# Low parts of the weights in four pieces, each with its own count, in a three-layer block kernel

## The reference, cut

```python
def reference(x, ...):
    h = rms_norm(x); proj = h @ w_in                 # pool, lru, q, k, v, three gates
    merged = g0 * (pool_mixer @ wb0) + g1 * (rglru_mixer @ wb1) + g2 * (stick_breaking_attention @ wb2)
    x = x + merged @ w_out
    x = x + (silu(rms_norm(x) @ w_gate) * (rms_norm(x) @ w_up)) @ w_down           # 1024 -> 2816 -> 1024
    # second model, layer 0: differential and block attention; layer 1: dilated and latent attention
    for layer in range(2):
        x = x + mixer(rmsnorm(x) @ w_in_layer) @ w_out_layer
        u, g = split(rmsnorm(x) @ ffn_w_in)
        x = x + (gelu(causal_conv3(g) + b) * u) @ ffn_w_out
    return rmsnorm(x)
```

## Time and profile before

| | us |
|---|---|
| three runs | 2345.93, 2337.33, 2343.05 |
| their median | 2343.05 |
| profiled execution, whole | 2347.11 |
| profiled execution, span of the trace | 2344.4 |
| PE busy | 2258.4 (96%) |
| POOL busy | 933.6 (40%) |
| DVE busy | 951.5 (41%) |
| ACT busy | 836.8 (36%) |
| granted TensorE clock, mean | 0.988 |

### The profile page before, as it was taken

The page is one execution under the profiler, slowest core; times in us unless marked ns, Lnnn a source line. Parts: engine busy times, 40 slices in busy tenths (PEclk is TensorE's granted clock), DMA queues, the critical chain, the costliest instruction groups (busy, mean ns, idle before and its releaser), DMA issues.

```text
span 2344.4 us, 27313 instructions
## 1 busy us (share of the span) xinstructions
PE 2258.4 (96%) x10130; PEld 1816.1 (77%) x10130; DVE 951.5 (41%) x1261; ACT 836.8 (36%) x1101; POOL 933.6 (40%) x264
## 2 busy tenths in 40 slices
PE   6999999899999999999988999999998999999997
PEld 4777877788878888888866778888886777888885
DVE  5244366634461111341156643233424546332334
ACT  4326465323232222331154333332323534333321
POOL 3331233443434344554421334436544123444453
PEclk9999999999999999999999999999998999999998
DMA  3221122222222322232321222222332112222232
GB/s 145 89 90 54 54 73 90 90 97 101 90 90 89 107 89 80 98 109 90 108 63 28 72 87 92 90 90 86 110 117 85 32 53 83 97 100 89 80 99 73
DMA packets 32701, 202.80 MB, mean 87 GB/s; under 512 B 3900, under 2 KB 4156, under 8 KB 13692
## 3 DMA queue, kind: packets, MB, share of 16 engines
q1 hardware_dynamic: 29932, 192.94, 23.8%
q0 software_dynamic: 2704, 8.97, 1.4%
HBM read 199.74 MB, written 2.15 MB: 86 GB/s over the span
## 4 chain that ended last, share of the span: by engine, by line
issue 53%; PE 30%; POOL 13%; DVE 1%; DMA 1%; ACT 0%; POOLq 0%; DVEq 0%; SPq 0%; ACTq 0%; PEldq 0%
POOL w_low L824 13%; PE bank L299 8%; PE bank L301 8%; PE bank L300 8%; PE bank L496 2%; PE bank L473 2%; PE bank L483 1%; DMA raw<-wmain 0%; PE bank L469 0%; PE bank L468 0%; POOLq L214 0%; DVE qk L1290 0%; DMA distance_table<-table 0%; PE bank L778 0%; PE bank L325 0%
## 5 line engine op out<-in xcount | busy, mean ns | idle before, releaser
L824 POOL TENSOR_TENSOR w_low<-raw,w_high 128x2048 fp32r<-128x2048 f32 x194 | 895.6, 4617 | 1249.3 <-ACT w_high L934 1236.9
L299 PE MATMUL bank<-x_low,w_high 128*128 128x512 f32 x1728 | 678.6, 393 | 17.2 <-DVE x_low L1283 9.2
L301 PE MATMUL bank<-x_high,w_low 128*128 128x512 f32 x1728 | 674.8, 391 | 0.0
L300 PE MATMUL bank<-x_high,w_high 128*128 128x512 f32 x1728 | 674.8, 390 | 0.0
L934 ACT ACTIVATE w_high<-raw 128x2048 fp32r<-128x2048 f32 x192 | 366.8, 1911 | 536.9 <-PE bank L301 532.8
L299 PEld LDWEIGHTS bank<-x_low,w_high 128*128 128x128 f32 x1728 | 325.5, 188 | 91.0 <-issue 20.0
L300 PEld LDWEIGHTS bank<-x_high,w_high 128*128 128x128 f32 x1728 | 325.7, 188 | 68.5 <-issue 1.2
L301 PEld LDWEIGHTS bank<-x_high,w_low 128*128 128x128 f32 x1728 | 325.5, 188 | 68.0
L299 PE MATMUL bank<-act_low,w_high 128*128 128x512 f32 x528 | 209.0, 396 | 1.3 <-POOL w_low L824 1.3
L301 PE MATMUL bank<-act_high,w_low 128*128 128x512 f32 x528 | 208.7, 395 | 0.0
L300 PE MATMUL bank<-act_high,w_high 128*128 128x512 f32 x528 | 208.6, 395 | 0.0
(11 more groups left out here) (239 smaller groups left out, 2458.8 us busy)
## 6 DMA issues: line engine op xcount, KB each, us to landing
raw<-wmain SPq DMA_DIRECT2D x146, 1024.0 KB, 4.8
raw<-wdown SPq DMA_DIRECT2D x48, 704.0 KB, 4.1
bias<-distance_table POOLq DMA_DIRECT2D x28, 256.0 KB, 3.4
x_residual<-x SPq DMA_DIRECT2D x2, 1024.0 KB, 6.1
out<-qk SPq DMA_DIRECT2D x8, 256.0 KB, 2.0
matrices<-mats SPq DMA_DIRECT2D x1, 512.0 KB, 9.9
r_blocks<-rg POOLq DMA_DIRECT2D x1, 512.0 KB, 6.4
i_blocks<-rg POOLq DMA_DIRECT2D x1, 512.0 KB, 7.0
```

What stands on the lines that cost most here:

```text
L299: pe.matmul(target, sh, ml, start=start and k == 0, stop=False)
L300: pe.matmul(target, sh, mh, start=False, stop=False)
L301: last = pe.matmul(target, sl, mh, start=False, stop=stop and k == n - 1)
L824: pool.tensor_tensor(wl[:, c, :], raw[:, c, :], wh[:, c, :].bitcast(F32), ALU.subtract).then_inc(low_ready, 1)
```

## The change

A constant `PIECES = 4` is new. POOL makes the low part of a chunk in four instructions, each with an increment of `low_ready`: of 512 columns each in a main chunk, of 384, 384, 384 and 256 in a down chunk. The first two chunks of each down stage are made in the last round of the stage ahead, as full ones with pieces of 512. All waits on `low_ready` count in pieces. PE waits for a piece where the first product of a chunk comes to it: every 2 steps in a main chunk, every step in a token-major one, every 3 in a down chunk. The second product of a chunk (`j` = 1, or the later token blocks) waits for none. The stage `qk` and the two chunks of `mla` still wait for the whole chunk through `chunk`. ACT's copy is 1408 columns wide where the chunk is a down chunk. The number of matmuls, loads and bytes is the same.

```diff
-                        sp_.wait_ge(low_ready, i * 2 + (n0 + c - 1))
+                        sp_.wait_ge(low_ready, i * (2 * PIECES) + PIECES * (n0 + c - 1))
...
                 for k, ((sh, sl), (mh, ml)) in enumerate(zip(stationary, moving)):
+                    if arrive and k % arrive[2] == 0:
+                        piece(arrive[0], arrive[1], k // arrive[2])
                     pe.matmul(target, sh, ml, start=start and k == 0, stop=False)
...
+            def piece(i, n, p):
+
+                pe.wait_ge(low_ready, i * PIECES + (PIECES * n + p + 1))
+
             def chunk(i, n):
-                pe.wait_ge(low_ready, i + (n + 1))
+
+                piece(i, n, PIECES - 1)
...
                 def part(i, n, c, x, read, x_ready=None):
-                    chunk(i * 2, n0 + 2 * n + c)
...
-                        products(bank[2 * c + j][:, :], weights(c, j), x).then_inc(sem(ready), 1)
+                        products(bank[2 * c + j][:, :], weights(c, j), x,
+                                 arrive=None if j else (i * 2, n0 + 2 * n + c, 2)).then_inc(sem(ready), 1)
...
-                chunk(0, BASE["mix"] + n)
                 for g in range(2):
                     f = 4 * c + 2 * g
+                    piece(0, BASE["mix"] + n, g)
...
-            def low(i, n, c):
+            def low(i, n, c, width=S):
 
                 pool.wait_ge(high_ready, i + (n + 1))
-                pool.tensor_tensor(wl[:, c, :], raw[:, c, :], wh[:, c, :].bitcast(F32),
-                                   ALU.subtract).then_inc(low_ready, 1)
+                for p in range(PIECES):
+                    part = slice(p * width, min((p + 1) * width, CHUNK if width == S else DOWN))
+                    pool.tensor_tensor(wl[:, c, part], raw[:, c, part], wh[:, c, part].bitcast(F32),
+                                       ALU.subtract).then_inc(low_ready, 1)
...
-                act.activation(wh[:, c, :], raw[:, c, :], ACT.Copy).then_inc(high_ready, 1)
+                act.activation(wh[:, c, 0:width], raw[:, c, 0:width], ACT.Copy).then_inc(high_ready, 1)
```

More of the change, by code:

```diff
@@ L333, in token_scales, with both_columns @@
                 last.then_inc(sem("token_scales"), 1)
-            def both_columns(c, x, read, target, ready, x_ready, at=0):
+            def both_columns(c, x, read, target, ready, x_ready, at, n):
                 for j in range(2):
@@ L340, in both_columns @@
                     pe.wait_ge(sem(x_ready[0]), x_ready[1] + k + 1)
+                    if k % 2 == 0:
+                        piece(0, n, k // 2)
                     for j in range(2):
@@ L356, in tiles @@
                     pe.wait_ge(sem(read), i * 4 + (2 * n + j + 1))
-                    products(bank[first + 2 * c + j][:, :], weights(c, j), x).then_inc(sem(ready), 1)
-                chunk(0, n0)
-                both_columns(0, x, read, first, ready, x_ready)
+                    products(bank[first + 2 * c + j][:, :], weights(c, j), x,
+                             arrive=None if j else (i * 2, n0 + n, 2)).then_inc(sem(ready), 1)
+                both_columns(0, x, read, first, ready, x_ready, 0, n0)
                 if norm:
                     norm_sum(norm)
-                chunk(0, n0 + 1)
                 tiles(0, 1, 1, 0)
@@ L403, in part @@
                 def part(i, n, c, x, read, x_ready=None):
[L404 removed]
                     if x_ready:
[L406 removed]
+                        both_columns(c, x, read, 2 * c, ready, x_ready, at, n0 + 2 * n + c)
                         return
@@ L430, in down @@
                         for c in range(2):
-                            chunk(i * 4, n0 + 2 * j + c)
                             pe.wait_ge(sem(x_ready), n * FT + (c + 1) * HALF)
                             products(bank[j][:, :], weights(c, 0, HALF, P), x[c * HALF:(c + 1) * HALF],
-                                     start=c == 0, stop=c == 1).then_inc(sem(ready), 1)
+                                     start=c == 0, stop=c == 1, arrive=(i * 4, n0 + 2 * j + c, 3))\
+                                .then_inc(sem(ready), 1)
             def turn(v, units, y_token):
@@ L574, in _ @@
                         last = products(bank[b][:, :], [(h[:, tokens], l[:, tokens]) for h, l in x], w,
-                                        start=c == 0, stop=c == 1)
+                                        start=c == 0, stop=c == 1,
+                                        arrive=None if b else (0, BASE["v"] + 2 * i + c, 1))
                         if c == 1 or b == NB - 1:
@@ L631, in column @@
                 n = MIX.index((kind, t // 2))
-                chunk(0, BASE["mix"] + n)
                 for k in range(KT):
+                    if t % 2 == 0 and k % 2 == 0:
+                        piece(0, BASE["mix"] + n, k // 2)
                     if x_ready:
@@ L830, in stage @@
                 rounds = count // 2 - (1 if n0 + count > CHUNKS else 0)
-                for i in repeat(pool, rounds):
-                    for c in range(2):
-                        low(i * 2, n0 + c, c)
+                down = count // 2 - 1 if name.startswith("down") else 0
+                if down:
+                    for i in repeat(pool, down):
+                        for c in range(2):
+                            low(i * 2, n0 + c, c, 3 * P)
+                if rounds > down:
+                    for i in repeat(pool, rounds - down):
+                        for c in range(2):
+                            low(i * 2, n0 + 2 * down + c, c)
             def query(kind, u0, i, n, u):
```

15 lines of the change are left out of this document (6 added, 9 removed).

## The result

| | before | after |
|---|---|---|
| median of the runs, us | 2342.38 (2337.33 to 2345.93, 4 runs) | 2323.62 (2320.39 to 2325.48, 4 runs) |
| profiled execution, us | 2347.11 | 2321.84 |
| span of its trace, us | 2344.4 | 2320.1 |
| mean granted clock in it | 0.988 | 0.993 |

The ratio of after to before is 0.992, with a 95% interval of 0.9897 to 0.9943. The predicted time was 2323.2 us. Between the medians lie 18.8 us, between the two spans 24.3, since the profiled execution of before was 4.7 us over its median and that of after 1.8 under.

The account below looks back on a forecast made before the run. PE, busy 96% of the span, bounds the kernel, so only its work and stalls can be won. Pieces 12.4 + DVE 5.4 + clock 2.6 - 0.6 = 19.8 us, giving 2323.2 us, range 2311 to 2335.

Parts of the forecast that it names:

- Gate and up entries: Second chunk pair of the three gate and up stages: PE's stalls for POOL's low part all go, 7.2 us.
- Down entries: First chunk of the three down stages: PE's stalls for POOL, each 0.6 us, all go, 1.8 us.
- A piece: POOL's time for a quarter of a chunk's low part: 1.23 us, with a fixed part of 0.10 us.
- a piece isn't a quarter: Rival, POOL's pieces: a fixed part of 1.4 us makes a piece 2.2 us; about 2350 us, chance 0.04.
- Pool products: Second chunk of the pool products: 3.4 us from the first piece, 1.5 us from DVE's chain ahead of ACT's copy.
- `x_low`: End of the three output projections: PE's waits for DVE's `x_low` go, 1.8 us (0 to 1.8).
- The start: Before PE's first product: two DVE operations slowed beside POOL gain 1.0 us (0 to 2.6).
- Dilated attention: DVE's operations behind POOL, for which PE stands, gain 1.1 us (0 to 3.4).
- The clock: Half-clock stretches after the third gate and up entry (1.6) and the pool products (1.0) go: 2.6 us (0 to 3.6).
- DVE comes first: Rival: back-to-back DVE operations keep the port, POOL takes what is left; 29 us gained, 2314 us, chance 0.20.
- Pieces alone: Rival: DVE stays blocked through all four pieces and clock dips stay; 11.8 us gained, 2331 us, chance 0.20.
- The waits show: Rival: PE's about 550 added waits hold up matmuls in gate, up and down loops; 2369 us, slower, chance 0.06.

Follow-up runs that it names:

- the repeat: The changed kernel run again unchanged, as the mark for the other runs: 2321.9 us, ratio 0.991 to the kernel before.
- Experiment 4: The changed kernel, but POOL makes a first piece, then the rest of the chunk in one instruction: 2331.78 us, ratio 0.9957 to the kernel before.
- experiment 3: The changed kernel with POOL's four pieces, but PE waits for the last piece of a chunk everywhere: 2346.13 us, ratio 1.0015 to the kernel before.
- experiment 1: The changed kernel with all of PE's new waits, but POOL makes each low part in one instruction: 2343.34 us, ratio 1.0001 to the kernel before.
- early high part: The changed kernel, but ACT makes the second pool product chunk's high part before its last `y_high` copy: 2321.39 us, ratio 0.9908 to the kernel before.

## Why the prediction was right, point by point

The forecast was the likeliest case, and it happened: PE starts on the first piece, and DVE gets turns. The sum without the clock's term was 17.2 us, and at an equal clock 16 were measured; the clock was worth 3 to 5 instead of 2.6. That the predicted median was met to 0.4 us is luck in part: these two errors cancel, and the middle of four runs shifts by 2 us with their clock (the repeat had 2321.9). Term by term, by how much earlier PE passes the same matmul in the two traces:

- **Gate and up entries**, predicted 7.2: 2.3, 2.7 and 2.6, together 7.6. **Down entries**, predicted 1.8: 0.7 each, 2.1. Right. Experiment 4 adds what the sum took for granted: it is not enough that a first piece is early, the following ones must come at PE's pace of 1.36 us. Without that, 3.8 us of waits come back.
- **A piece**, estimated at 1.23 us, took 1.29, and 384 columns 1.02, not 0.95. From 256, 384 and 512 columns (0.74, 1.02, 1.29) the fixed part comes to 0.19 us, not the 0.10 of a memset. The rival "a piece isn't a quarter" needed 1.4.
- **Pool products**, predicted 3.4 + 1.5 = 4.9: 4.5. The size is right, the remaining wait is not what I said. "PE's wait for `w_low`, 2 to 5 us, all before the pool products" is there with 3.7 us, but for `y_low` from DVE. I had not looked at what else PE needs at that matmul.
- **`x_low`** at the output projections, predicted 1.8: 0.7 each, 2.1, a little over what I took as the most; the 1.3 us of waits are gone. Right, and experiments 3 and 4 show that it is the turns. L1336's mean, which I gave as the sign of it, is a poor one: in experiment 4 it is 0.96 us, lower than in the changed kernel, and PE waits as before.
- **The start**, predicted 1.0 gained: 0.3 lost. This is the one term with the wrong sign. I wrote myself that a DVE chain without gaps wins little if they take turns, and then still took 1.0 for it. Each of the three instructions had to wait for a piece.
- **Dilated attention**, predicted 1.1: 1.5 (the wait for `probs` fell from 6.3 to 4.8). The first instruction took 1.34 us instead of 4.58, but the two behind it 3.42 instead of 1.69: each of them now waited for a piece.
- **The clock**, 2.6: the 1.6 after the third entry came. Of the 1.0 after the pool products 0.4 came, as the stall stayed at 3.7 us. The premise, that without a stall nothing pulls the clock down, holds at the gate and up entries. Whether more stalls gone explain the 3 to 5 us between the medians isn't shown.
- **The waits**, taken as 0: 0, by experiment 1. **POOL's later end**, 0.6 lost before the attentions: POOL's last chunk there ends 0.4 us later against PE's last product; what it costs PE can't be separated from the clock around it.

Without the clock the terms come to 17.5 us in these two traces. Of the 24.3 between their spans, 2.5 are slow stretches that are shorter or gone at the start, after the pool products and after the third entry. Another 2.3 lie in the first attention and about 1 just ahead of the dilated one, places where before has one half-clock stretch more each. The prediction has no term for them. The stretch ahead of the dilated attention isn't the change's doing: in the repeat's trace it is there again (0.50 at 1760.1). For the first attention it stays open.

Of the rivals, "DVE comes first" is out: at the start two DVE instructions took 3.46 us. "Pieces alone" would have left `x_low` and `probs` as they were. "The waits show" is out by experiment 1. The Trainium skill, "SBUF — State Buffer", section "Summary: rules for kernel authors", says of a DVE instruction with two SBUF inputs beside a GpSimd one that reads SBUF that the second to issue fully blocks until the first finishes; the traces agree but for about 0.2 us of overlap, at each of the three lengths of POOL's instruction compared (5.08 us behind 4.55, 1.8 behind 1.29, 1.2 behind 0.74, where DVE alone takes 0.7).

## What to carry to other kernels

Cutting a producer's instruction brings two separate things: the consumer can start on the first part, and whoever shares the producer's port gets a turn. Check for the first that the later parts keep the consumer's pace, for the second that the blocked engine's work has gaps; a chain without gaps pays a piece per instruction, and is better kept apart in time. Before a stall is booked as gone, list everything that its matmul waits for: the next cause may be right behind.

## What the runs showed of the hardware

- POOL and DVE took strict turns when both had work queued: DVE's instructions of 0.7 us took 1.73 to 1.82 beside pieces of 512 columns, about 1.2 beside pieces of 256. Cutting POOL's work thus makes POOL's own chunk longer, 5.96 us against 4.55 at the second gate and up entry (without DVE beside it four pieces took 5.02).
- The mean granted clock of a run, 0.988 to 0.994 for one and the same kernel, went with 2347.7 to 2337.0 us. A difference of 5 us between two kernels is better read at an equal clock than from medians of three or four runs.
- The length of a stall alone did not tell whether the granted clock fell behind it. Of the stalls of PE looked at here, those of 0.7, 1.6 and 1.6 us (experiment 4), 2.0 and 2.4 (first and second entry before) and 3.0 (early high part) were not followed by a lower clock; those of 2.2 (eight pieces, pool products), 2.4 (third entry before), 2.8, 3.7 and 3.7 (experiment 3), 3.7 (after) and 8.3 (before) were. Each is one execution.
